# V's lower parts all on VectorE, its weights by two chunks, and blocks of U and V read two at a time in 8192-byte runs

## The reference

```python
q = (xt @ w_q).reshape(T, PEER_HEADS, 2, PEER_DK_HALF)
s = jnp.einsum('thpd,hpnd->thpn', q, sub_keys).astype(jnp.float32)
...
top_s, pos = lax.top_k(cand, PEER_TOPK)
idx = jnp.take_along_axis(cand_idx, pos, axis=-1)
gates = jax.nn.softmax(top_s, axis=-1).astype(x.dtype)
...
u = u_table[ic]
a = jax.nn.gelu(jnp.einsum('cd,ced->ce', xc, u), approximate=False) * gc
return jnp.einsum('ce,ced->cd', a, v_table[ic])
```

## Time and profile before

| | |
|---|---|
| median of 3 runs | 1675.98 us |
| the profiled execution | 1681.09 us, its span 1679.0 us |
| stage U, by TensorE's first matmuls | about 524 to 1117 us of the span |
| stage V | about 1117 to 1664 us |
| TensorE busy over the span | 96% |
| VectorE busy over the span | 81% |
| GpSimd busy over the span | 65% |

### The profile page before, as it was taken

The page is one execution under the profiler, slowest core; times in us unless marked ns, Lnnn a source line. Parts: engine busy times, 40 slices in busy tenths (PEclk is TensorE's granted clock), DMA queues, the critical chain, the costliest instruction groups (busy, mean ns, idle before and its releaser), DMA issues. The chain is left out here.

```text
span 1679.0 us, 26370 instructions
## 1 busy us (share of the span) xinstructions
PE 1616.1 (96%) x9763; PEld 1494.6 (89%) x9763; DVE 1360.1 (81%) x2450; ACT 752.5 (45%) x1342; POOL 1092.8 (65%) x620
## 2 busy tenths in 40 slices
PE   9999999999999989999999999989999899999996
PEld 7788877788889989999999999989999899899896
DVE  7876636744524899999998789769999899999995
ACT  6533326544213333446767887533333333333333
POOL 4544422344434889987766678988787687787872
PEclk9999999999999999999999999999999999999999
DMA  8322332374445999999888899999999999999991
GB/s 225 101 76 71 106 99 58 91 243 138 115 118 159 330 336 349 367 331 327 321 325 294 335 406 372 388 330 366 382 376 375 367 364 368 375 389 371 377 359 63
DMA packets 241256, 459.26 MB, mean 274 GB/s; under 512 B 15905, under 2 KB 156449, under 8 KB 239593
## 3 DMA queue, kind: packets, MB, share of 16 engines
q1 hardware_dynamic: 137416, 200.38, 36.1%
q0 software_dynamic: 46080, 167.79, 26.1%
q10 hardware_dynamic: 57632, 89.41, 14.8%
HBM read 402.31 MB, written 55.18 MB: 272 GB/s over the span
## 5 line engine op out<-in xcount | busy, mean ns | idle before, releaser
L283 POOL TENSOR_TENSOR spl_a<-raw,spl_a 128x1024 fp32r<-128x1024 f32 x232 | 594.8, 2566 | 282.3 <-ACT spl_a L279 280.3
L279 ACT ACTIVATE spl_a<-raw 128x1024 fp32r<-128x1024 f32 x294 | 309.5, 1054 | 272.4 <-PE bank L291 209.1
L289 PE MATMUL bank<-x_dense,spl_a 128*128 128x352 f32 x1024 | 337.1, 329 | 8.1 <-ACT gl L1579 6.8
L291 PE MATMUL bank<-x_dense,spl_a 128*128 128x352 f32 x1024 | 330.5, 323 | 0.0
L290 PE MATMUL bank<-x_dense,spl_a 128*128 128x352 f32 x1024 | 329.8, 322 | 0.0
L1852 DVE SCALAR_TENSOR_TENSOR hot<-rows,a_row,hot 128x1024 f32<-128x1024 f32 x157 | 310.7, 1997 | 0.0
L289 PE MATMUL bank<-aws,spl_a 128*128 128x352 f32 x768 | 255.6, 333 | 32.3 <-DVE aws L1832 30.5
L1357 POOL DMA_INDIRECT rows<-in_v_tab,expert x160 | 220.5, 1378 | 45.2 <-issue 34.6
L290 PE MATMUL bank<-aws,spl_a 128*128 128x352 f32 x768 | 249.7, 325 | 0.0
L291 PE MATMUL bank<-aws,spl_a 128*128 128x352 f32 x768 | 249.6, 325 | 0.0
L1357 POOL DMA_INDIRECT rows<-in_u_rows,expert x160 | 165.8, 1036 | 68.5 <-DVE rows L1368 35.1
(11 more groups left out here) (358 smaller groups left out, 3127.3 us busy)
## 6 DMA issues: line engine op xcount, KB each, us to landing
raw<-in_u_t SPq DMA_DIRECT2D x128, 512.0 KB, 5.5
raw<-in_v_tab SPq DMA_DIRECT2D x128, 512.0 KB, 7.0
dense_gates<-mixbuf ACTq DMA_DIRECT2D x11, 2048.0 KB, 11.2
mixbuf<-dense_gates ACTq DMA_DIRECT2D x16, 1408.0 KB, 23.1
raw<-in_w_in SPq DMA_DIRECT2D x42, 512.0 KB, 3.9
gelu_ux<-gl ACTq DMA_DIRECT2D x120, 176.0 KB, 5.7
mixbuf<-gelu_ux ACTq DMA_DIRECT2D x30, 704.0 KB, 10.7
raw<-in_w_q SPq DMA_DIRECT2D x16, 512.0 KB, 4.1
```

What stands on the lines that cost most here:

```text
L279: eng.activation(spl(n, 0, slice(0, W)), raw[:, s, :], ACT.Copy).then_inc(hi_done, 1)
L283: eng.tensor_tensor(spl(n, 1, slice(0, W)), raw[:, n % RAW, :], spl(n, 0, slice(0, W)).bitcast(F32), ALU.subtract) \
L289: nc.tensor.matmul(out, w_hi, x_hi, start=first, stop=False)
L291: return nc.tensor.matmul(out, w_lo, x_hi, start=False, stop=last)
```

## The change

Six things change together.

1. `by_vector` is true for every unit of V from `V0 + LEAD` on: GpSimd makes no lower part of those any more, VectorE makes all.
2. `weight`, `weight_hi` and `weight_lo` take two chunks at once, 704 columns instead of 352. `AWS` is 4 instead of 3, and `FIRST_UNITS` 4 instead of 3.
3. The last 32 dot products read a copy of their tokens in PSUM: VectorE waits for the 128 dot products before them, and copies `x_copies` over `x_rows`.
4. Two neighbouring blocks are loaded in one DMA (`paired`), 8192 bytes for each partition. For that U is laid out in HBM by partition and then unit (`u_t`). The pair waits until both its slots are free.
5. Some small buffers take other places (`pair_i` in PSUM, `iota_f` inside `hot`, three rows inside `dot_rows`).
6. The tables of places are written anew, mostly one or two units later; the dot products at the end of stage U are spread a little differently.

```diff
-AWS = 3
+AWS = 4
...
+        def pair_source(n):
+            if n < V0:
+                return u_t[:, n - U0:n - U0 + 2, :]
+            c = expert_chunk(n - V0)
+            return v_tab[:, c:c + 2, :]
+
+        def paired(n):
+
+            if n % 2 or n < U0 or n + 1 >= N_UNITS or n < V0 <= n + 1:
+                return False
+            return n < V0 or expert_chunk(n + 1 - V0) > expert_chunk(n - V0)
+
+        def loader(n):
+
+            return n - 1 if paired(n - 1) else n
+
         def by_vector(n):
 
-            return n in VECTOR_LO or (n >= V0 + LEAD and (n - V0 - LEAD) % 2 == 0)
+            return n in VECTOR_LO or n >= V0 + LEAD
...
+            elif paired(n):
+                wait_lo(sp, n + 1 - RAW)
+                sp.dma_start(raw[:, s:s + 2, :], pair_source(n)).then_inc(unit_loaded[s], 16)
...
-            GATHER_AT = [4, 4, 4, 5, 6, 6, 7, 8, 8, 9, 10, 11, 11, 12, 13, 13, 14, 15, 16, 17, 18, 18, 20, 21, 22,
...
+            GATHER_AT = [4, 4, 4, 5, 6, 7, 7, 8, 9, 9, 10, 11, 11, 12, 13, 14, 14, 15, 17, 17, 18, 19, 20, 21, 22,
...
-            FIRST_UNITS = 3
+            FIRST_UNITS = 4
...
-                    if j % 2 and V0 + LEAD + j < N_UNITS:
-                        split_lo(pool, V0 + LEAD + j)
                     for s in value_steps(j):
                         if s + ROWS < STEPS:
                             gather(pool, STEPS + s + ROWS)
...
+                def weight_hi(b):
+                    act_e.wait_ge(a_mult, b + 1)
+                    if b >= 2:
+                        act_e.wait_ge(unit_used, V0 + 2 * b - 2)
+                    act_e.activation(aws[:, 0, b % 2 * 2:b % 2 * 2 + 2, :], aw[:, b % 2, :, :], ACT.Copy).then_inc(a_hi, 1)
...
                         if g == SLOTS:
                             dve.wait_ge(rows_copied, 2)
-                        u_dot(dve, g, x_rows[:, :, :].rearrange("p b t -> p (b t)") if g < SLOTS else x_copies)
+                            dve.wait_ge(row_used, SLOTS)
+                            mark(dve.tensor_copy(x_rows[:, :, :].rearrange("p b t -> p (b t)"),
+                                                 x_copies.rearrange("p k c -> p (k c)")))
+                            settle()
+                        u_dot(dve, g, x_rows[:, :, :].rearrange("p b t -> p (b t)"))
...
                 weight_lo(0)
                 weight_lo(1)
-                weight(2)
-                dots(LAST_DOTS[1])
-                weight_lo(2)
-                dots(LAST_DOTS[2])
+                dots(LAST_DOTS[1] + LAST_DOTS[2])
...
-                    if FIRST_UNITS <= j + 2 < NC:
-                        weight(j + 2)
+                    if j % 2 == 0 and FIRST_UNITS <= j + 2 < NC:
+                        weight(j // 2 + 1)
                     for s in value_steps(j):
                         add_row(STEPS + s)
-                    if FIRST_UNITS <= j + 2 < NC:
-                        weight_lo(j + 2)
-                    if j % 2 == 0 and V0 + LEAD + j < N_UNITS:
+                    if j % 2 == 0 and FIRST_UNITS <= j + 2 < NC:
+                        weight_lo(j // 2 + 1)
+                    if V0 + LEAD + j < N_UNITS:
                         split_lo(dve, V0 + LEAD + j)
...
-        "u_t": c(peer_u[0].reshape(NK, NC, KD, P).transpose(1, 3, 2, 0).reshape(NC, P, W)),
+        "u_t": c(peer_u[0].reshape(NK, NC, KD, P).transpose(3, 1, 2, 0).reshape(P, NC, W)),
```

More of the change, by code:

```diff
@@ L204, in build @@
         tiles = sb(outer, "tiles", [P, 2, KD, P])
-        outer.enter_context(nc.sbuf_tensor("act_rest", [P, 2 * KD * (T - DT - P)], F32))
+        dot_rows = sb(outer, "dot_rows", [P, 2 * KD * (T - DT - P)])
+        z_row, g_row, a_row = [dot_rows[:, i * STEPS:(i + 1) * STEPS] for i in range(3)]
         first_half = ExitStack()
@@ L247, in load_unit @@
         def load_unit(sp, n):
+            if loader(n) != n:
+                return
             if n >= RAW:
@@ L261, in load_unit, with loads_before @@
                     .then_inc(unit_loaded[s], 16)
+            elif paired(n):
+                wait_lo(sp, n + 1 - RAW)
+                sp.dma_start(raw[:, s:s + 2, :], pair_source(n)).then_inc(unit_loaded[s], 16)
             else:
                 sp.dma_start(raw[:, s, :], unit_source(n)).then_inc(unit_loaded[s], 16)
-        def loads_before(n, s):
-            return sum(2 if BR0 <= m < WO0 else 1 for m in range(s, n + 1, RAW))
+        def loads_before(n):
+            return sum(2 if BR0 <= m < WO0 else 1 for m in range(loader(n) % RAW, n + 1, RAW) if loader(m) == m)
         def last_step(n):
@@ L1418, in build @@
             place = bank[3][:, 3 * P:3 * P + 2 * TOPK].bitcast(U32).rearrange("p (a k) -> p a k", a=2)
+            pair_i = bank[3][:, 3 * P + 2 * TOPK:3 * P + 4 * TOPK].bitcast(U32).rearrange("p (a k) -> p a k", a=2)
             span = rank_f[:, :, 0, :].bitcast(U32)
@@ L1425, in build @@
             TAIL_STEPS = 32
[L1426 to L1429, removed]
+            TAIL_QUADS = 33
+            TAIL_DOTS = 33
+            LATE_STEPS = 15
+            LATE_DOTS = 15
             SCORES_AT = [0, 0, 0, 8, 14, 19, 24, 30, 35, 41, 46, 52, 58, 64, 70, 76]
-            EXP_AT = [21, 44, 69, 92]
-            SLOTS_AT = [None, 47, 71, 97]
-            GATHER_AT = [4, 4, 4, 5, 6, 6, 7, 8, 8, 9, 10, 11, 11, 12, 13, 13, 14, 15, 16, 17, 18, 18, 20, 21, 22,
[6 rows of a table removed]
+            EXP_AT = [21, 45, 69, 93]
+            SLOTS_AT = [None, 48, 72, 98]
+            GATHER_AT = [4, 4, 4, 5, 6, 7, 7, 8, 9, 9, 10, 11, 11, 12, 13, 14, 14, 15, 17, 17, 18, 19, 20, 21, 22,
[6 rows of a table added]
             PAIR_DOTS = [0, 4, 8, 6, 7, 7, 7, 7, 7, 8, 6, 6, 6, 6, 6, 6]
-            PAIR_QUADS = [0, 0, 0, 0, 0, 0, 0, 0, 0, 5, 5, 6, 6, 8, 8, 8]
+            PAIR_QUADS = [0, 0, 0, 0, 0, 0, 0, 0, 0, 5, 5, 6, 7, 8, 8, 8]
             LAST_DOTS = [3, 3, 3]
@@ L1814, in slots_out, with weight, weight_lo @@
                     settle()
-                def weight(j):
-                    half = j // 4 % 2
+                def weight(b):
+                    j = 2 * b
+                    part, group = j // 4, j // 8
                     if j % 8 == 0:
-                        dve.wait_ge(gates_mixed[j // 8 % 2], 16 * (j // 16 + 1))
+                        dve.wait_ge(gates_mixed[group % 2], 16 * (group // 2 + 1))
                     if j >= KEPT and j % 4 == 0:
-                        dve.wait_ge(gelu_mixed[half], 16 * (j // 8))
+                        dve.wait_ge(gelu_mixed[part % 2], 16 * (j // 8))
                     if j < KEPT:
-                        dve.wait_ge(z_free, NC - KEPT + j + 1)
-                    if j >= 2:
-                        dve.wait_ge(a_lo, j - 1)
-                    dve.tensor_tensor(aw[:, j % 2, :].rearrange("p (b t) -> p b t", t=TB),
-                                      gelu_in[:, half, j % 4, :].rearrange("p (b t) -> p b t", t=TB),
-                                      gates_in[:, j // 8 % 2, :, j % 8, :], ALU.mult).then_inc(a_mult, 1)
-                def weight_lo(j):
-                    dve.wait_ge(a_hi, j + 1)
-                    dve.tensor_tensor(aws[:, 1, j % AWS, :], aw[:, j % 2, :], aws[:, 0, j % AWS, :].bitcast(F32),
-                                      ALU.subtract).then_inc(a_lo, 1)
+                        dve.wait_ge(z_free, NC - KEPT + j + 2)
+                    if b >= 2:
+                        dve.wait_ge(a_lo, b - 1)
+                    dve.tensor_tensor(aw[:, b % 2, :, :].rearrange("p c (b t) -> p b c t", t=TB),
+                                      gelu_in[:, part % 2, j % 4:j % 4 + 2, :].rearrange("p c (b t) -> p b c t", t=TB),
+                                      gates_in[:, group % 2, :, j % 8:j % 8 + 2, :], ALU.mult).then_inc(a_mult, 1)
+                def weight_lo(b):
+                    at = slice(b % 2 * 2, b % 2 * 2 + 2)
+                    dve.wait_ge(a_hi, b + 1)
+                    dve.tensor_tensor(aws[:, 1, at, :], aw[:, b % 2, :, :], aws[:, 0, at, :].bitcast(F32), ALU.subtract) \
+                        .then_inc(a_lo, 1)
                 def add_row(g):
```

35 lines of the change are left out of this document (11 added, 24 removed), and 30 rows, old and new, of tables (EVICT_AT, GATHER_AT, QUAD_AT, SCALE_AT).

## The result

The changed kernel takes 1682.6 us (median of 7 runs, 1675.2 to 1693.5), the kernel before in the same job 1675.6 us (median of 7, 1674.1 to 1680.5). The ratio is 1.005, with an interval of 1.0027 to 1.0073: slower by 0.5%. The forecast was 1658.

The account below looks back on a forecast made before the run. VectorE was taken to bound stage V, largely by waits inside its instructions, with DMA close behind. Stage V -16, between the stages -6, loads in stage U +4 gave -18 us: 1658 us, range 1643 to 1684 (the forecast case's own 1650 to 1668).

Parts of the forecast that it names:

- VectorE in stage V: Stage V stretch: splits +65 us, additions -106, weights -7; VectorE needs 416 us instead of 463.7, no longer the bound.
- What stands next in stage V: Stage V after VectorE's relief: DMA sets 4.05 us a unit instead of 4.19, -16 us; bounds 3.92 and 4.19.
- The rest of that step: Stage V's DMA limit: share 1.03 gives 387 GB/s, 4.03 us a unit, 3.99 with wider runs, before 0.06 for refills.
- TensorE's own pace: Stage V with TensorE alone as bound: 3.92 us a unit, -31 us.
- Rival 1: Stage V: TensorE becomes the bound at 3.92 to 3.95 us a unit, 1645 us; chance 0.15.
- Between the stages: Start of stage V: shorter dot products and wide weights bring TensorE's unit 4 forward, -6 us, bounds 0 and -9.
- late loads in U: Stage U: three pairs of blocks land later and hold up ScalarE's gelu, +4 us, bounds 0 and +12.
- Rival 2: Stage V: DMA was the bound all along, pace stays 4.15 to 4.19 us a unit, 1674 us; chance 0.15.
- Rival 3: Stage V: gates and gelu refills starve beside wider block packets, 1704 us; chance 0.15, shared with late loads in stage U.
- What had been named as a sign of being wrong: VectorE releasing TensorE after full work, ScalarE awaiting blocks in many units, or `weight` awaiting `mixbuf` every eight units.

Follow-up runs that it names:

- the two other versions with early refills: Changed kernel with refills two units earlier and blocks loaded singly, all of them or only U's: 1652.0 us each, ratio 0.984 each.
- the kernel with early refills: Changed kernel with refills of gates and gelu issued two units earlier, blocks still in pairs: 1652.9 us, ratio 0.986 to the kernel before.

## Why the prediction was wrong

**VectorE in stage V: right.** The forecast was 416 us for the window; it is 403.7. The additions brought 108 us (106 forecast) and the splits cost 70 (65). The weights brought 28 instead of 7: before, some of the narrow ones had been held up too (549 and 576 ns on average, where a free one shows 510), which the sum had left out. A wide weight takes 0.80 us from start to start (1304.04 to 1304.84 in the timeline after), as worked out, and the additions take the free 1278 ns. The rule that an instruction of VectorE with two inputs in SBUF contends with one of GpSimd that reads SBUF (the Trainium skill, SBUF — State Buffer, Who interferes with whom) agrees with the 1575 and 1521 ns that come back with GpSimd's splits.

**What stands next in stage V: the step that failed.** Its last line adds 0.06 us a unit, 7 us in all, for refills that are asked for sooner; the whole gain of 16 us hung on that. The pace stayed at 4.21, so late refills and what follows from them cost 0.22 us a unit over the 3.99 of the sum, some 25 us in place of 7. In the trace after, the four long waits before weights are 3.8 + 8.0 + 7.0 + 4.4 = 23 us, and the lower clock behind a stop is paid on top: (102 - 87) / 102 of 16 us, 2.4 us in the window shown. I priced the refill by how late it already was, and not by how much sooner it would be asked for. That could be computed. Gelu for chunks 8g+16 on is issued at unit 8g+10 and needed at 8g+14. Four units were 16.8 us at 4.19 and are 15.3 at the 3.82 that TensorE runs at between the stops; the gelu issued at 1298.69 had 14.3. It lies on one queue behind 1408 KB of gates, which have 704 KB of gelu just ahead of them, and landed after 22.3.

The semaphore events in the trace of before give the landings that such a sum needs. Its gelu issued at units 8g+10 took 17.7, 13.2, 15.6, 13.7, 19.2, 5.9, 15.7, 13.1, 10.7, 14.4, 18.4 and 14.0 us from 1165 to 1560 us. The three over 16.8 are the ones that VectorE waited for, 2.2, 5.8 and 2.9 us, nearly all of the 11.2 of the earlier trace rows (which put them down to issue). Five are over 15.3, and six over the 14.3 that was left. So the number of late refills about doubles, even if none takes longer than before.

Why the long stops came every second group between 1250 and 1459, and why none came later, is open. Part of an explanation shows in the trace: during a stop the DMA empties (share 0.66), and the gelu issued right behind the four stops landed in 4.5 to 5.5 us, where the median is 11.2. That this alone sets the rhythm was only argued.

**The rest of that step: right.** With refills in time the pace is 4.00 at 393 GB/s; the step had 387 GB/s, and 3.99 ahead of the 0.06. How close that came is in part luck: the two other versions with early refills ran at 4.05. The DMA is then most likely the bound, at a share that I had called sustainable from a window of 20 us. The profiled runs of before and of the kernel with early refills are 28.7 us apart, the medians 22.4; the forecast was 18.

**TensorE's own pace** was taken as 3.92 us from one pair of units; without the gates' later loads it is 3.84. Rival 1 was thereby priced too high, 1645 where 1635 is the floor that the runs show. It plays no part in the failure.

**Between the stages and late loads in U.** -6 and +4 were forecast for unit 4, and -7.2 measured in one pair of traces. The dot products take 1.21 us as said. Unit 4 came 14.6 us behind the last of them instead of 8, since the first addition waited 4.1 us for its row and the split behind it 2.4 us for ScalarE, but the gates landed 5.4 us earlier. With pairs V unit 0 begins at 1114 to 1120 in five traces, with single blocks at 1107.1 and 1109.8; but with pairs in V alone it is 1115.6, and the medians with early refills are equal. What the wide loads cost or bring stays open; it is less than the measurement tells.

**The rivals.** Rival 2, that the DMA was the bound all along, gives the measured size and falls all the same: 393 GB/s over 445 us with 1.4% less time. Nor does the figure of about 358 GB/s for a core (the Trainium skill, DMA: Bandwidth & Descriptors, Where 436 GB/s comes from) hold as a limit here, where one core ran: 366 to 393 were sustained in stage V. Rival 3 had the place right (starved refills, and each of them a matter of some 4 us, the gain gone from four or five on), and the cause wrong: it blamed the blocks' wider packets, yet with single loads the waits for gelu were longer, with late refills (47.5 us against 24.4) and with early ones (26.2 against 0.6). What the runs with early refills point to is the time from issue to use.

**What had been named as a sign of being wrong** is what came: the weight waits for `mixbuf`, for long every 16 units from 1250 to 1459 us, where eight were named. ScalarE also waits for blocks, 37 times and 107 us; with early refills, where it is 132 us, this is the form in which the DMA's bound shows.

The best versions are the whole change with early refills, with pairs or without: 1652.0 to 1652.9 us, 1.4 to 1.6% less than before.

## What to carry to other kernels

When a change takes the bound away, list every transfer that is issued at a fixed step of the loop, and compare its landing time, behind what lies on the same queue, with the steps between issue and use at the new pace. Take the spread of the landing times, not the median: here the median was 11 us, and it was the ones of 14 to 22 us that counted. A stop of the slow engine is paid twice, once as a wait and once in clock and transfer rate. Issue a refill at the instruction that frees its buffer; if the change moves that instruction forward, as the wide weights did by one unit (from 4p+1 to 4p), move the issue with it, and take the slack of one unit that was there before.

## What was not expected of the hardware

- The DMA engines held 393 GB/s for 445 us at a share of 1.02, with gathers, blocks and refills on three queues (the kernel with early refills).
- After 7.45 us without a matmul TensorE's granted clock was 0.87 over the next 16 us. In the trace of after four stops of TensorE of 3.75 to 7.45 us went with a pace no better than before (4.207 against 4.203), though VectorE had 60 us less to do.
- Runs of 8192 bytes do travel as larger packets (18003 packets fewer), but time didn't follow: 1652.9 us with them, 1652.0 without. What they moved was the waiting: from the refills to the blocks.
- A multiplication of 704 columns whose inputs are in SBUF took 885 ns where GpSimd had no splits and 1521 ns on average beside its splits.
